# Order and owners of a few splits and loads in a decoder layer: upper token half first, two feature splits and the MLP weight sums on GpSimd, down-product loads in another order

## What is computed

```python
    p = causal_pool_mixer(xp, pool_w[l], pool_scale[l])
    y_attn = jnp.einsum('bsa,ad->bsd', a.reshape(B, S, ATTN_WIDTH), w_up_attn[l])
    y_pool = jnp.einsum('bsp,pd->bsd', p, w_up_pool[l])
    merged = gates[:, :, 0] * y_attn + gates[:, :, 1] * y_pool
    x = x + jnp.einsum('bsd,de->bse', merged, w_o[l])

    h2 = rms_norm(x, norm2_g[l])
    u = jnp.square(jax.nn.relu(jnp.einsum('bsd,df->bsf', h2, w_mlp_in[l])))     # D_FF = 4096
    x = x + jnp.einsum('bsf,fd->bsd', u, w_mlp_out[l])
```

## Time and profile before

| what | us |
|---|---|
| median of 3 runs | 1310.71 (1309.72 to 1311.17) |
| the profiled execution | 1309.64 |
| its span, first to last instruction | 1307.3 |
| TensorE busy | 1269.4 (97%) |
| VectorE busy | 889.5 (68%) |
| ScalarE busy | 534.0 (41%) |
| GpSimd busy | 358.5 (27%) |
| mean granted TensorE clock | 0.995 of full |

### The profile page before, as it was taken

How to read it: one execution, slowest core, us unless ns; L and a number is a source line. 1 busy time by engine, 2 the same in 40 slices (tenths; PEclk the granted TensorE clock), 3 DMA queues, 4 the chain that set the end, 5 groups by cost and what they waited for, 6 DMA issues and landing times.

```text
span 1307.3 us, 17648 instructions
## 1 busy us (share of the span) xinstructions
PE 1269.4 (97%) x6153; PEld 1063.6 (81%) x6153; DVE 889.5 (68%) x1234; ACT 534.0 (41%) x936; POOL 358.5 (27%) x375
## 2 busy tenths in 40 slices
PE   5999999999899999999999999999998999999998
PEld 5889888887688888887888788888886888888887
DVE  5778777778722222245478877877867998978964
ACT  5556555555311111142245544544454333333330
POOL 3334334333400000000002323332434821606025
PEclk9999999999899999999999999999998999999999
DMA  8010100101111111115222445444539626253223
GB/s 262 17 49 18 44 21 20 36 0 49 33 49 48 48 48 48 64 64 177 81 95 92 155 150 169 150 141 161 168 141 383 245 102 221 96 196 130 95 99 138
DMA packets 106813, 140.65 MB, mean 108 GB/s; under 512 B 4461, under 2 KB 62466, under 8 KB 106754
## 3 DMA queue, kind: packets, MB, share of 16 engines
q1 hardware_dynamic: 106754, 139.88, 31.6%
HBM read 102.12 MB, written 37.75 MB: 107 GB/s over the span
## 4 chain that ended last, share of the span: by engine, by line
PE 86%; DVE 7%; issue 3%; ACT 2%; DMA 1%; POOL 0%; SPq 0%; DVEq 0%; ACTq 0%; POOLq 0%
PE bank L1588 79%; PE bank L1756 2%; PE bank L1685 2%; PE bank L1644 1%; DMA o_raw<-in_w_mlp_out 1%; DVE slot_lo L1049 1%; DVE featT_lo L1330 1%; DMA raw<-in_w_in 1%; ACT slot_hi L712 1%; DVE c L1509 1%; DVE pair_lo L1437 1%; PE bank L1863 1%; PE bank L1739 0%; DVE mixT_lo L1266 0%; DVE wT_lo L1140 0%
## 5 line engine op out<-in xcount | busy, mean ns | idle before, releaser
L1588 PE MATMUL bank<-o_hi,s_hi 128*128 128x512 f32 x448 | 175.5, 392 | 4.8 <-DVE o_lo L1450 4.8
L1588 PE MATMUL bank<-o_hi,s_lo 128*128 128x512 f32 x448 | 175.2, 391 | 0.0
L578 POOL TENSOR_SCALAR small<-small 128x1 f32<-128x1 f32 x80 | 21.2, 265 | 537.4 <-ACT h_row L979 339.0
L1049 DVE TENSOR_TENSOR slot_lo<-raw,slot_hi 128x1024 fp32r<-128x1024 f32 (+1 forms) x45 | 55.2, 1235 | 140.0 <-ACT slot_hi L712 139.5
L1588 PE MATMUL bank<-featT_hi,slot_hi 128*128 128x512 f32 x320 | 127.4, 398 | 0.0
L1588 PE MATMUL bank<-featT_lo,slot_hi 128*128 128x512 f32 x320 | 125.4, 392 | 0.0
L1588 PE MATMUL bank<-featT_hi,slot_lo 128*128 128x512 f32 x320 | 125.1, 391 | 0.0
L1588 PE MATMUL bank<-slot_hi,featT_hi 128*128 128x384 f32 (+1 forms) x320 | 117.9, 368 | 7.3 <-DVE slot_lo L1049 5.3
L1588 PE MATMUL bank<-slot_lo,featT_hi 128*128 128x384 f32 (+1 forms) x320 | 111.7, 349 | 0.0
L1588 PE MATMUL bank<-slot_hi,featT_lo 128*128 128x384 f32 (+1 forms) x320 | 111.5, 349 | 0.0
L1588 PEld LDWEIGHTS bank<-o_hi,s_hi 128*128 128x128 f32 x448 | 84.6, 189 | 23.1 <-DVE o_lo L1450 5.2
(11 more groups left out here) (196 smaller groups left out, 3173.3 us busy)
## 6 DMA issues: line engine op xcount, KB each, us to landing
s_raw<-u_store SPq DMA_DIRECT2D x28, 1024.0 KB, 5.6
pair_raw<-in_w_mlp_in SPq DMA_DIRECT2D x16, 1024.0 KB, 6.1
u_store<-s_tile SPq DMA_DIRECT2D x64, 256.0 KB, 2.1
o_raw<-in_w_mlp_out SPq DMA_DIRECT2D x16, 1024.0 KB, 8.5
raw<-in_w_in SPq DMA_DIRECT2D x28, 512.0 KB, 4.1
...
```

The lines of the kernel that those rows point to most:

```text
L578: pool.tensor_scalar(ms, ss, 1.0 / n_mean, EPS, ALU.mult, ALU.add).then_inc(mean_sem, 1)
L1049: nc.vector.tensor_tensor(slot[1][:, 0:width], raw[r][:, 0:width], slot[0][:, 0:width], ALU.subtract).then_inc(w_ready, 1)
L1588: mm = nc.tensor.matmul(out, a, b, start=start and i == 0, stop=stop and i == len(steps) - 1)
```

## The change

- In the loop over d, the up-projections and merges of the upper token half (tokens 512 to 1023) come first. For the last block (k = 7), `mergedT` is split in two halves: the upper one as soon as it is merged, the lower one after the split of block WO+6 on DVE. The output projection waits for the upper half at its first tile, for the lower one at its second.
- The lo parts of features k = 3 and k = 5 (two subtractions of 1024 elements) go from DVE to POOL, counted by a new semaphore `m_by_pool`.
- The four sums of the weights of pairs 2 to 15 (`t_sums`) go from DVE to POOL, where they stand ahead of the four `s_tile` sums of the pair two earlier. DVE's lo splits of P5 and P6 now also wait for the sum that reads what they overwrite.
- The `o_raw` blocks of quarter 0 get other places and another order of loads: block 0 already after pair 14's splits, block 3 after pair 15's, block 1 after product P6 of pair 15, block 2 after P7. Of `acc`, four blocks are loaded there and four with `s_raw` 3.

```diff
@@ -147,10 +148,10 @@
-        O_PLACES = ((184, 88, 96, 200), (128, 136, 144, 152))
+        O_PLACES = ((192, 96, 88, 200), (128, 136, 144, 152))
...
-        o11_lo = at("o11_lo", 192, [P, 4, HT], F32R)
+        o11_lo = at("o11_lo", 184, [P, 4, HT], F32R)
@@ -472,7 +473,8 @@
             load_wo(7, 2, 4)
-            sp.wait_ge(m_split, KD)
+            sp.wait_ge(m_split, KD - 1)
+            sp.wait_ge(m_by_pool, 2)
             sp.dma_start(g2_row[:], norm2_g.to_broadcast([P, D])).then_inc(g2_in, 16)
@@ -510,28 +517,29 @@
                 if p + 2 < PAIRS:
                     sp.wait_ge(t_ready, turn(p, P3))
                     load_pair(p + 2)
+                if p == PAIRS - 2:
+                    sp.wait_ge(t_ready, turn(p, P3))
+                    load_o(0, 0)
                 if p == PAIRS - 1:
                     sp.wait_ge(p_done, turn(p, P1))
                     load_s(1)
                     sp.wait_ge(p_done, turn(p, P6))
-                    load_o(0, 2)
+                    load_o(0, 1)
                     sp.wait_ge(p_done, turn(p, P2))
                     load_s(2)
                 sp.wait_ge(u_ready, 4 * p + 1)
                 store_u(D1, p, u_tile[0])
                 if p == PAIRS - 2:
                     sp.wait_ge(t_ready, 7 * PAIRS)
+                    load_o(0, 3)
                     sp.wait_ge(p_done, turn(p, P3))
-                    load_o(0, 0)
                     load_s(0)
-                    load_o(0, 3)
                 if p == PAIRS - 1:
-                    sp.wait_ge(p_done, turn(p, P7))
-                    load_o(0, 1)
                     for i in range(3):
                         sp.wait_ge(res_out[i], 16 * (3 - i // 2))
-                    for t in range(T):
-                        sp.dma_start(acc[:, t, :], res_store[t]).then_inc(acc_in[t // QN], 16)
+                    load_acc(0)
+                    sp.wait_ge(p_done, turn(p, P7))
+                    load_o(0, 2)
                 sp.wait_ge(u_ready, 4 * p + 3)
                 store_u(D4, p, u_tile[2])
                 for i, q in enumerate((D7, D5, D6)):
@@ -550,6 +558,8 @@
                     load_o(c + 1, (3, 1, 0, 2)[i - 2])
                 if n > 2:
                     load_s(n)
+                if n == 3:
+                    load_acc(1)
             for t in range(QN):
                 sp.wait_ge(folded, 3 * QN + t + 1)
                 sp.dma_start(y_rows[QN + t], acc[:, QN + t, :]).then_inc(y_out, 16)
@@ -648,11 +658,30 @@
             wide_sums(2, range(3))
 
 
+            for n, k in enumerate((3, 5)):
+                pool.wait_ge(m_hi, k + 1)
+                pool.tensor_tensor(featT[1][:, k, :], mergedT[:, k, :], featT[0][:, k, :], ALU.subtract).then_inc(m_by_pool, 1)
             for s in range(T):
                 x_inverse(s, r_squared, r_mean, r_inv)
 
             u11, u21, u22, u12 = u_tile
+
+            def t_sums(p):
+
+                b11, b12, b21, b22 = (b_quarter(p, q) for q in range(4))
+                f = pair_f[p % 2]
+                pool.wait_ge(pair_in[p % 2], 16 * (p // 2 + 1))
+                pool.wait_ge(p_done, turn(p - 2, P3))
+                pool.tensor_tensor(f[:, P5], b12, b11, ALU.subtract).then_inc(t_f, 1)
+                pool.wait_ge(t_f, 4 * p + 1)
+                pool.tensor_tensor(f[:, P6], f[:, P5], b22, ALU.subtract).then_inc(t_f, 1)
+                pool.wait_ge(t_f, 4 * p + 2)
+                pool.tensor_tensor(f[:, P4], b21, f[:, P6], ALU.add).then_inc(t_f, 1)
+                pool.tensor_tensor(f[:, P7], b22, b12, ALU.subtract).then_inc(t_f, 1)
+
             for p in range(PAIRS):
+                if p + 2 < PAIRS:
+                    t_sums(p + 2)
                 pool.wait_ge(u_ready, 4 * p + 2)
                 wait(pool, u_out[1], 16 * p)
                 pool.tensor_tensor(s_tile[0][:], u11[:], u21[:], ALU.subtract).then_inc(s_ready, 1)
@@ -910,20 +939,21 @@
                     next_tile(d, g)
 
 
-            def merged_hi(k):
-
-                act.wait_ge(merged_ready, 2 * k + 2)
-                nc.scalar.activation(featT[0][:, k, :], mergedT[:, k, :], ACT.Copy).then_inc(m_hi, 1)
+            def merged_hi(k, half, ready):
+
+                act.wait_ge(merged_ready, ready)
+                nc.scalar.activation(featT[0][:, k, half], mergedT[:, k, half], ACT.Copy).then_inc(m_hi, 1)
 
             split_hi(WO + 2, 3, HEADS + 2, slots[WO_SLOT[2]], mix_full, 2 * GROUPS)
             act.wait_ge(gate_full, 4 * KD)
             for k in range(KD - 1):
-                merged_hi(k)
+                merged_hi(k, ALL, 2 * k + 2)
+            merged_hi(KD - 1, HALVES[1], 2 * KD - 1)
             split_hi(WO + 3, 2, PIECES[2] * (HEADS + KD + 1), slots[WO_SLOT[3]], up_full, 4 * KD)
-            merged_hi(KD - 1)
-            for b, (r, loads) in enumerate(((0, HEADS + KD + 2), (1, HEADS + KD + 2), (3, HEADS + 3),
-                                            (2, PIECES[2] * (HEADS + KD + 1) + 1))):
-                split_hi(WO + 4 + b, r, loads, slots[4 + b])
+            split_hi(WO + 4, 0, HEADS + KD + 2, slots[4])
+            merged_hi(KD - 1, HALVES[0], 2 * KD)
+            for b, (r, loads) in enumerate(((1, HEADS + KD + 2), (3, HEADS + 3), (2, PIECES[2] * (HEADS + KD + 1) + 1))):
+                split_hi(WO + 5 + b, r, loads, slots[5 + b])
 
             def copy_hi(dst, src):
 
@@ -1319,34 +1350,36 @@
 
             with dve.Fori(1, KD - 1) as d:
                 tile_weights(d)
-                for i in range(2):
-                    merge(d, 0, i, 2 * i)
-                    merge(d, 1, i, 2 * i + 1)
-
-
-            def merged_lo(k):
-
-                dve.wait_ge(m_hi, k + 1)
-                nc.vector.tensor_tensor(featT[1][:, k, :], mergedT[:, k, :], featT[0][:, k, :], ALU.subtract).then_inc(m_split, 1)
+                for i in (1, 0):
+                    merge(d, 0, i, 2 - 2 * i)
+                    merge(d, 1, i, 3 - 2 * i)
+
+
+            def merged_lo(k, half, nth):
+
+                dve.wait_ge(m_hi, nth)
+                nc.vector.tensor_tensor(featT[1][:, k, half], mergedT[:, k, half], featT[0][:, k, half],
+                                        ALU.subtract).then_inc(m_split, 1)
 
             last = KD - 1
             tile_weights(last)
             split_lo(WO + 2, 3, slots[WO_SLOT[2]])
-            merged_lo(0)
-            merged_lo(1)
-            merge(last, 0, 0, 0)
-            merged_lo(2)
-            merged_lo(3)
-            merge(last, 1, 0, 1)
-            merged_lo(4)
-            merged_lo(5)
-            merge(last, 0, 1, 2)
-            merged_lo(6)
-            merge(last, 1, 1, 3)
+            merged_lo(0, ALL, 1)
+            merged_lo(1, ALL, 2)
+            merge(last, 0, 1, 0)
+            merged_lo(2, ALL, 3)
+            merge(last, 1, 1, 1)
+            merged_lo(4, ALL, 5)
+            merge(last, 0, 0, 2)
+            merged_lo(6, ALL, 7)
+            merged_lo(last, HALVES[1], 8)
+            merge(last, 1, 0, 3)
             split_lo(WO + 3, 2, slots[WO_SLOT[3]])
-            merged_lo(last)
-            for b, r in enumerate((0, 1, 3, 2)):
-                split_lo(WO + 4 + b, r, slots[4 + b])
+            split_lo(WO + 4, 0, slots[4])
+            split_lo(WO + 5, 1, slots[5])
+            split_lo(WO + 6, 3, slots[6])
+            merged_lo(last, HALVES[0], 9)
+            split_lo(WO + 7, 2, slots[7])
 
             def add_res(s, i):
 
@@ -1412,28 +1445,22 @@
                 b11, b12, b21, b22 = (b_quarter(p, q) for q in range(4))
                 f = pair_f[par]
                 out = (P5, P6, P4, P7)[k]
-                dve.wait_ge(pair_in[par], 16 * (p // 2 + 1))
-                if p > 1:
-                    dve.wait_ge(p_done, turn(p - 2, P3))
-                else:
-                    wo_leaves(dve, p, out)
+                dve.wait_ge(pair_in[par], 16)
+                wo_leaves(dve, p, out)
                 if k in (1, 2):
                     dve.wait_ge(t_f, 4 * p + k)
                 a, b, op = ((b12, b11, ALU.subtract), (f[:, P5], b22, ALU.subtract), (b21, f[:, P6], ALU.add),
                             (b22, b12, ALU.subtract))[k]
                 nc.vector.tensor_tensor(f[:, out], a, b, op).then_inc(t_f, 1)
 
-            def t_sums(p):
-
-                for k in range(4):
-                    t_sum(p, k)
-
             def t_split_lo(p, i):
 
                 par = p % 2
                 f = pair_f[par]
                 src = (f[:, P5], f[:, P4], b_quarter(p, 0), f[:, P6], b_quarter(p, 2), f[:, P7], b_quarter(p, 3))[i]
                 dve.wait_ge(t_hi, turn(p, i))
+                if p > 1 and i in (P5, P6):
+                    dve.wait_ge(t_f, 4 * p + {P5: 2, P6: 3}[i])
                 nc.vector.tensor_tensor(pair_lo[par][:, i], src, pair_hi[par][:, i], ALU.subtract).then_inc(t_ready, 1)
 
             def down_lo_o(n):
@@ -1497,7 +1524,6 @@
                     for i in range(2, 5):
                         t_split_lo(1, i)
                 elif more:
```

(8 more changed lines are left out.)

10 lines of the change are left out of this document (7 added, 3 removed).

## The result

The changed kernel takes 1317.05 us (median of 20 runs, 1310.19 to 1321.73), the kernel before 1310.73 (1308.36 to 1312.14): ratio 1.0049, 95% interval 1.0036 to 1.0061. It is slower by 6.3 us. Forecast were 1311.7, a range up to 1316.0, and "the same" as the likeliest; the time lies 1 us above the range.

A forecast was written before the change was run, and what follows sets the result against it. TensorE, busy 97% of the span, was taken as the bound, so only holes in its rhythm could be won. Terms +1.8 + 2.5 + 1.0 - 4.3 = +1.0 us gave 1311.7 us, range 1307.2 to 1316.0.

The forecast's parts named there:

- three holes: TensorE idle at the output projection (2.2 us), before pair 2's P4 (1.7 us) and before `down_product(1)` (4.8 us).
- nothing to win in the steady pairs: Moving work off DVE in the steady part of the first MLP half was claimed to win nothing.
- What sharing costs: DVE and POOL instructions with two SBUF inputs go one after the other; 1024 elements take POOL 2.40 us alone.
- Rival (1): No mutual wait of DVE and POOL at the three holes: together -8.5 us, 1302.2 us; chance 0.09.
- A: Start of the output projection: POOL's two subtractions hold up DVE, so the lo part of WO+3 comes later: +1.8 us.
- Rival (2): The granted clock falls in the longer holes, slowing the first 11 matmuls after each: +4.5 us, 1315.2 us; chance 0.26.
- B: Pair 2's P4: DVE's splits alternate with POOL's sums, bank free 2.5 us later, plus 1.0 us for a fallen clock.
- The second burst on POOL: In pair 2, POOL's weight sums for pair 3 meet DVE's two late splits, holding the second up by 1.1 us.
- The later pairs: Pairs after pair 2: DVE's splits end later but within the allowed time, so no hole and no gain: 0 us.
- its sign of being wrong: DVE's durations beside POOL staying at 0.68 and 1.22 us, or a new hole appearing in the steady pairs.
- C: Handover to the down product: earlier loads restart TensorE 2.7 us sooner, later `s_lo` waits shrink too: -4.3 us in all.
- Sum: Adds +1.8, +2.5, +1.0 and -4.3 to +1.0 us on the profiled execution; on the median 1311.7 us.

The follow-up runs named there:

- e7: Kernel before with the new down-product loads, pair loads issued early, and weight sums on POOL only from pair 4 on: 1307.52 us, ratio 0.9975.
- e2: Changed kernel with the weight sums of all pairs back on DVE, the rest kept: 1309.86 us, ratio 0.9994.
- e1: Changed kernel with SP issuing the load of the next pair's weights ahead of the `s_tile` stores, not behind them: 1313.42 us, ratio 1.0026.
- e12: Changed kernel with pair loads issued early and the weight sums of pairs 2 and 3 back on DVE: 1309.72 us, ratio 0.9991.
- e4: Kernel before with only the weight sums of pairs 2 to 15 moved to POOL: 1317.74 us, ratio 1.0053.
- e3: Kernel before with only the new order and places of the down-product loads: 1307.55 us, ratio 0.9973.

## Why the prediction was wrong, step by step

- **What bounds the kernel; three holes; nothing to win in the steady pairs.** Right (e7: sums moved off DVE, no gain).
- **What sharing costs.** Right, and it carried every number that held. POOL took 2.42 us for the first 1024 elements (taken: 2.40), DVE 3.13 and 2.16 us beside it (forecast 3.2 and 2.2; the estimate of 2.2 us for POOL that stood beside the 2.40 was too low), 1.77 for 512 elements, 3.3 for 2048. Rival (1), no mutual wait, falls.
- **A, +1.8.** Right: the restart for WO+3 came 1.7 us later in all five traces with this code, and its halves and its feature splits measured apart give 0.6 + 1.1 = 1.7. The whole term was +1.5 to +1.8 where the clock held (two traces of the changed kernel, e2) and +2.2 and +3.3 where it fell (e1, e12). Rival (2) had 0.4 for that.
- **B, +2.5 and +1.0 for the clock.** The size was roughly right, 4.4 instead of 3.5, by two errors of opposite sign. The second burst on POOL did not come, since the load of pair 3 was late (hole +1.7, not +2.5); where the load was early it came as counted (+2.8, e1). And the clock cost 2.7 us instead of 1.0. In the four traces with POOL's sums in pair 2 it fell every time, for 2.7, 2.7, 1.6 (e4) and 1.4 us (e1, though its hole was the longest). So the term of +1.0 was too small in each, and that 4.4 lies near 3.5 is in part luck.
- **The later pairs: "no hole, no gain. The cover is 1.9 us thick."** This is the step that failed: +4.0 us instead of 0. I went through DVE's queue with the `s_tile` sums "some 4 us later" and asked only when ACT wants them. I did not ask who else waits for them: SP, which stores them and has the next pair load queued behind the last store. The rows of before show SP's order; I had read SP at the handover alone. The other half of the circle was in the diff: POOL waits for that load ahead of the `s_tile` sums. Shown by e1 (this order alone, pairs back to 19.04 us) and e4 (the sums alone, circle there). A new hole in the steady pairs is also what the prediction had named as its sign of being wrong.
- **C, -4.3.** The restart was sized rightly: 2.8 us earlier in e1, e2, e3 and e7. The rest of the term was mostly the fall of the clock in the kernel before (2.2 us by its count), taken not to come again. That the kernel before "waited for `s_lo` 2" is a misreading: its TensorE has no idle time at 1020.4, though `s_lo` 2 had ended only 0.1 us before (row below, PE busy 11.00 us of 11). Two things were off. The clock fell after the hole of 2.0 us ("holes of that size kept the clock"), which leaves -2.8 to -3.0 in the four kernels without the circle; rival (2) had this at -2.4. The further gain was real only where the clock held (e12, -5.0), and then `s_lo` 5 took it back. And in the changed kernel the circle had delayed pair 14's last `s_tile` sum until it ran beside `o_lo` 0, so `s_raw` 1 was issued at 993.79, behind its store, and ACT's and DVE's chain began 2 us late: -1.0 in all.

```profile
1020.00:1031.00 11.00, 11.00 (x50) 8.98 (x49) 9.64 (x10) 5.02 (x3) 7.36 (x4) 1.00 1.05 384
```

- **Sum.** As measured, the terms give 1.8 + 4.4 + 4.0 - 1.0 = +9.2 in the trace, 9.7 with the 0.5 from the first stage; the medians differ by 6.3. The two traced executions of the changed kernel lie 1.7 and 1.3 us above their medians, that of the kernel before 1.1 under its own; the 20 times of the changed kernel reach from 1310.2 to 1321.7. Times and clock go together: the four runs with the highest mean clock (0.997) took 1310.2 to 1313.3, the others (0.993 to 0.995) 1314.4 to 1321.7.
- **The range.** Its lower end, 1307.2, does not follow from the bounds as stated: A +0.8, B -1.8 and C -4.3 give -5.3 and 1305.4. The time lay above the upper end, so nothing hangs on it.
- **Rivals.** (2) was part of what happened: 2.7 us in B and 1.7 in C. The one that decided, the circle, was not on the list: of "an engine that waits for another" I had only looked for cases within DVE, POOL and TensorE.

What stays open: why the clock falls after some holes and not after others of the same length; and which of the two forms of the pairs' loss (even, or late and abrupt) is the usual one, since two traces show one of each.
